# Router logits taken from unscaled rows, the last tile routed alone, and expert loads, gate table and output stores placed anew in a two-layer diffusion backbone block

## The reference, cut to what matters

```
u = modulate(rmsnorm(h, norm_mix[l]), m_lat[0], m_lat[1])
...
h = h + m_lat[2] * y
v = modulate(rmsnorm(h, norm_ffn[l]), m_lat[3], m_lat[4])
lg = (xt @ w_grp + b_grp)
le = (xt @ w_exp + b_exp).reshape(T, N_GROUPS, EXP_PER_GROUP)
...
y = (silu(xb @ w1[e]) * (xb @ w3[e])) @ w2[e]
h = h + m_lat[5] * f
...
return rmsnorm(h, norm_final)
```

## Time and profile before

| | |
|---|---|
| time, median of 3 runs | 2534.87 us (2527.97 to 2536.31) |
| profiled execution: its time, its span | 2530.3 us, 2528.4 us |
| mean granted TensorE clock | 0.973 |
| PE busy | 2361.4 us (93%) |
| DVE, ACT, POOL busy | 1092.6, 338.2, 158.2 us |
| DMA | 574.19 MB, mean 227 GB/s |

### The profile page before, as it was taken

The page is one execution under the profiler, slowest core; times in us unless marked ns, Lnnn a source line. Parts: engine busy times, 40 slices in busy tenths (PEclk is TensorE's granted clock), DMA queues, the critical chain, the costliest instruction groups (busy, mean ns, idle before and its releaser), DMA issues. The chain is left out here.

```text
span 2528.4 us, 32830 instructions
## 1 busy us (share of the span) xinstructions
PE 2361.4 (93%) x14163; PEld 1049.8 (42%) x14164; DVE 1092.6 (43%) x2145; ACT 338.2 (13%) x669; POOL 158.2 (6%) x179
## 2 busy tenths in 40 slices
PE   5999999989999999999999799999999999999991
PEld 3455444544545533333333444444555333333330
DVE  2688377757846422222222453343563222222225
ACT  2210333321011100000000320000120000000001
POOL 2000000001000000000000000000000000000000
PEclk8999999999999999999999899999998999999996
DMA  9567100120120799999999611111019999999975
GB/s 330 200 235 253 34 25 26 47 79 33 67 92 34 299 359 405 405 391 407 392 397 373 223 56 33 50 64 36 34 59 331 387 401 403 404 394 407 387 301 230
DMA packets 186892, 574.19 MB, mean 227 GB/s; under 512 B 14783, under 2 KB 39591, under 8 KB 151544
## 3 DMA queue, kind: packets, MB, share of 16 engines
q1 hardware_dynamic: 168648, 526.48, 54.7%
q0 software_dynamic: 18016, 45.31, 4.7%
q10 hardware_dynamic: 80, 0.26, 0.0%
HBM read 550.74 MB, written 38.03 MB: 233 GB/s over the span
## 5 line engine op out<-in xcount | busy, mean ns | idle before, releaser
L1637 PE MATMUL ps<-arena 128*32 128x512 f32 x6144 | 678.7, 594 | 7.1 <-DMA arena<-in_ex_w_dram 6.5
L1637 PEld LDWEIGHTS ps<-arena 128*32 128x32 f32 x6144 | 193.4, 110 | 423.8 <-issue 423.0
L1663 PE MATMUL ps<-arena 128*32 128x512 f32 x3072 | 338.7, 592 | 5.6 <-DMA arena<-in_ex_w_dram 5.6
L2364 DVE TENSOR_SCALAR arena<-ps,gain_x,mod 128x128 f32<-128x128 f32 x384 | 126.9, 403 | 373.4 <-PE ps L1622 373.4
L1766 PE MATMUL ps<-arena 128*128 128x512 f32 x616 | 264.5, 592 | 0.0
L1507 PE MATMUL ps<-arena 128*128 128x512 f32 x512 | 226.4, 596 | 1.6 <-DVE arena L2166 1.6
L1663 PEld LDWEIGHTS ps<-arena 128*32 128x32 f32 x3072 | 105.1, 110 | 230.1 <-issue 230.1
L2396 DVE SCALAR_TENSOR_TENSOR arena<-ps,arena,gates 128x512 f32<-128x512 f32 x96 | 72.1, 751 | 256.3 <-PE ps L1663 256.3
L1766 PEld LDWEIGHTS ps<-arena 128*128 128x128 f32 x616 | 117.0, 190 | 147.3 <-issue 147.3
L1322 PE MATMUL ps<-arena 128*128 128x512 f32 x384 | 167.3, 593 | 0.7 <-issue 0.7
L2372 DVE TENSOR_TENSOR arena<-arena,ps 128x512 f32<-128x512 f32 x48 | 52.7, 1098 | 239.8 <-PE ps L1637 239.8
(11 more groups left out here) (304 smaller groups left out, 2136.9 us busy)
## 6 DMA issues: line engine op xcount, KB each, us to landing
arena<-in_ex_w_dram SPq DMA_DIRECT2D x384, 1024.0 KB, 11.7
arena<-in_mod_w_dram SPq DMA_DIRECT2D x24, 2048.0 KB, 8.8
arena<-expert_rows SPq DMA_DIRECT2D x16, 1024.0 KB, 8.8
arena<-in_od_w_in_dram SPq DMA_DIRECT2D x12, 1024.0 KB, 5.2
arena<-in_x_dram SPq DMA_DIRECT2D x2, 4096.0 KB, 14.7
normed_rows<-arena POOLq DMA_DIRECT2D x16, 512.0 KB, 2.9
arena<-in_ev_w_in_dram SPq DMA_DIRECT2D x3, 2048.0 KB, 13.6
arena<-in_ev_w_in_dram SPq DMA_DIRECT2D x12, 512.0 KB, 4.1
```

The source lines that it names most:

```text
L1637: ins = nc.tensor.matmul(bank(2 + m)[c:c + n], x[:, j, c:c + n], w_slot(e % 2, m, KC, FE)[:, j], start=j == 0, stop=j == KC - 1)
L1663: ins = nc.tensor.matmul(bank(5 + half)[c:c + n], HT[:, j * P + c:j * P + c + n], w_slot(e % 2, 2, FC, D)[:, j, half * 512:(half + 1) * 51 ...
L2364: ins = V.tensor_scalar(XT[:, b, j * P:(j + 1) * P], bank(j // 4)[:, (j % 4) * P:(j % 4 + 1) * P], gain_x[:, 2 * l + 1, j:j + 1], mod[:, l ...
```

## The change

At the start, tiles 0 and 1 are turned ahead of the fourth modulation matmul (with other PSUM banks for the modulation), and the other tiles one in the middle and one at the end of each tile of v. In routing, PE turns H itself, unscaled, with every eighth element of a row as a chunk; the router's weights are multiplied by the gain once, the shift's part of the logits is added to the router's bias by eight matmuls with ones (`SHIFTED`), and the row's scale is applied to the logits as they are read. ACT makes the scaled rows for the gather table. Logits of tile i-1 stand in the middle of the second half of tile i, their routing ahead of that half's residual; tile 6 is placed before the last tile's transposes are read. In the experts, one weight matrix of expert 0 is loaded before routing, and expert 1's second and third behind the first gather; w2 comes in halves of its inner rows, and the down-projection goes over both column halves in each inner chunk; the gate table is made behind the first pass's gate matmuls; ACT writes half of the first XT. The output stores no longer wait for the last tile's sum. The diff, cut to what carries this (semaphore counts of other norms and a bank number in `rows_to_columns` are left out), outdented by eight:

```diff
@@ -233,6 +233,7 @@
 XN, VTT, SQ_OUT = at(12288, 2, D), at(14336, 2, KC * P), at(16384, 2, D)
+SHIFTED = at(15360, KC, NG + NE)
 HT, SL, HS = at(31232, FE), at(31744, FE), at(30720, FE)
...
@@ -431,6 +432,8 @@
 root_base = [sum(ROOTS[:n]) for n in range(len(ROOTS) + 1)]
+SCALES = [1, 2 * TT, TT, 2 * TT, TT]
+scale_base = [sum(SCALES[:n]) for n in range(len(SCALES) + 1)]
...
@@ -483,6 +486,9 @@
+def halves_before(l, p):
+    return 3 * NP * l + max(3 * p - 1, 0)
+
 def w_slot(b, m, *dims):
...
@@ -524,22 +530,30 @@
                 if m == 2:
-                    cs = slice(half * 512, (half + 1) * 512)
-                    dst = w_slot(e % 2, m, FC, D)[:, :, cs]
-                    src = srcs[m][l, e].rearrange("(p j) n -> p j n", p=P)[:, :, cs]
+                    js = slice(half * 2, half * 2 + 2)
+                    dst = w_slot(e % 2, m, FC, D)[:, js]
+                    src = srcs[m][l, e].rearrange("(p j) n -> p j n", p=P)[:, js]
                 else:
...
+        if l:
+            sp.wait_ge(od_done, 3 * NQ)
+            weights(0, 1)
+        else:
+            sp.wait_ge(hmix_ready, 2 * HC)
+            weights(0, 2)
+        sp.wait_ge(h_ready, 2 * TT * (l + 1))
+        sp.wait_ge(xn_ready, norm_base[2 * l + 2])
         weights(0, 0)
         weights(1, 0)
-        weights(0, 1)
-        weights(0, 2)
+        weights(0, 2 if l else 1)
         sp.wait_ge(lg_mm, TT * (l + 1))
...
         sp.wait_ge(hn_out[1], 16 * (TT // 2) * (l + 1))
+        sp.wait_ge(x_full[0], 16 * (l * NP // 2 + 1))
         weights(1, 1)
...
@@ -548,17 +562,19 @@
                 for m, mm in ((0, up_mm), (1, gate_mm)):
-                    sp.wait_ge(half_mm, 2 * (n0 + p) + m + 1)
+                    sp.wait_ge(half_mm, halves_before(l, p) + m + 1)
                     for e in freed:
...
             if freed_down:
-                for half in range(2):
-                    sp.wait_ge(y_mm, 2 * (n0 + p) - 1 + half)
-                    for e in freed_down:
-                        weights(e, 2, (half,))
+                sp.wait_ge(half_mm, halves_before(l, p) + 3)
+                for e in freed_down:
+                    weights(e, 2, (0,))
+                sp.wait_ge(y_mm, n0 + p)
+                for e in freed_down:
+                    weights(e, 2, (1,))
...
@@ -666,15 +682,12 @@
-        sp.wait_ge(h_ready, 2 * TT * (l + 1))
-        sp.wait_ge(xn_ready, norm_base[2 * l + 2])
         moe_weights(l)
-        sp.wait_ge(y_mm, 2 * NP * (l + 1))
+        sp.wait_ge(y_mm, NP * (l + 1))
         sp.wait_ge(tab_ready, l + 1)
...
         combine(l)
-    sp.wait_ge(cy_used, 2 * TT)
     for i in range(TT):
...
@@ -989,7 +1002,7 @@
     for i in range(TT + CT):
-        nxt = min(3 * (i + 1), TT + CT)
+        nxt = min(2 * i + 3, TT + CT)
         columns(0, lambda i, j: U[:, j, i * P:(i + 1) * P] if i < TT else UC[:, j, (i - TT) * P:(i - TT + 1) * P],
...
@@ -1082,35 +1095,53 @@
         n = 2 * l + 1
-        nb, rb = norm_base[n], root_base[n]
-
-        def columns_of(i):
-            act.wait_ge(xn_T, nb + i + 1)
-            if i >= 2:
-                act.wait_ge(lg_mm, l * TT + i - 1)
-            for j in range(KC // 2, KC):
-                ins = nc.scalar.activation(
-                    VTT[:, i % 2, j * P:(j + 1) * P], bank(5)[:, (j - 4) * P:(j - 3) * P], ACT.Identity,
-                    scale=gain_x[:, n, j:j + 1], bias=mod[:, l, 3, j:j + 1])
-            ins.then_inc(u_act, 1)
-
-        for i in range(TT):
-            if i:
-                columns_of(i - 1)
+        nb, sb_ = norm_base[n], scale_base[n]
+
+        def square(i):
             act.wait_ge(h_ready, 2 * TT * l + 2 * (i + 1))
...
                 .then_inc(sq_done, 1)
-            act.wait_ge(ms_ready, rb + i + 1)
+
+        def root(i):
+            act.wait_ge(ms_ready, sb_ + 2 * i + 1)
             nc.scalar.activation(rstd[:, i:i + 1], rstd[:, i:i + 1], ACT.Sqrt).then_inc(root_ready, 1)
-        columns_of(TT - 1)
+
+        def scaled(i):
+            act.wait_ge(ms_ready, sb_ + 2 * i + 2)
+            if i >= 2:
+                act.wait_ge(hn_out[i % 2], 16 * (l * (TT // 2) + i // 2))
+            nc.scalar.activation(XN[:, i % 2].rearrange("t (c p) -> t p c", p=P),
+                                 H[:, i].rearrange("t (p c) -> t p c", c=KC), ACT.Identity,
+                                 scale=rstd[:, i:i + 1]).then_inc(xn_ready, 1)
+
+        def columns_of(i):
+            act.wait_ge(xn_T, nb + i + 1)
+            if i >= 2:
+                act.wait_ge(lg_mm, l * TT + i - 1)
+            nc.scalar.activation(VTT[:, i % 2, 512:], bank(5), ACT.Copy).then_inc(u_act, 1)
+
+        for i in range(TT):
+            if i:
+                columns_of(i - 1)
+            square(i)
+            if i == TT - 1:
+                columns_of(i)
+            root(i)
+            scaled(i)
         act.wait_ge(gexp_in, 2 * l + 1)
...
     def experts(l):
+        act.wait_ge(x_T, 2 * (l * NP + 1))
+        for j in range(KC // 2, KC):
+            ins = nc.scalar.activation(
+                XT[:, 0, j * P:(j + 1) * P], bank(1)[:, (j - 4) * P:(j - 3) * P], ACT.Identity,
+                scale=gain_x[:, 2 * l + 1, j:j + 1], bias=mod[:, l, 3, j:j + 1])
+        ins.then_inc(xt_ready, 1)
         for p in range(NP):
...
@@ -1192,13 +1223,15 @@
                 g = 32 * (j % 4)
-                ins = nc.tensor.matmul(bank(n % 2)[g:g + 32], SILU32[:, j], w[:, j],
+                ins = nc.tensor.matmul(bank((3, 6)[n % 2])[g:g + 32], SILU32[:, j], w[:, j],
                                        start=j < 4, stop=j >= 4)
...
                 fold(0)
+                for i in range(2):
+                    transposes(0, i, at(41984, 2, D))
         fold(1)
...
@@ -1231,11 +1264,8 @@
         w = slab(L0_V, KC, GV)
-        turned = 0
+        turned = 2
         for i in range(TT + CT):
-            while turned < min(3 * (i + 1), TT + CT):
-                transposes(0, turned, at(41984, 2, D))
-                turned += 1
             if i == 0:
...
@@ -1245,7 +1275,13 @@
                                        start=j == 0, stop=j == KC - 1)
+                if j == 3 and turned < TT + CT:
+                    transposes(0, turned, at(41984, 2, D))
+                    turned += 1
             ins.then_inc(v_mm, 1)
+            if turned < TT + CT:
+                transposes(0, turned, at(41984, 2, D))
+                turned += 1
             if i == 6 or i == 9:
...
@@ -1504,18 +1540,23 @@
             for j in range(KC):
+                if j == KC // 2 and i and half:
+                    logits(i - 1)
                 ins = nc.tensor.matmul(bank(m % 4), mixed[:, j, i * P:(i + 1) * P],
...
         def turn_rows(i):
-            pe.wait_ge(xn_ready, nb + i + 1)
+            pe.wait_ge(h_ready, 2 * TT * l + 2 * (i + 1))
             if i:
...
                 pe.wait_ge(u_act, nb + i)
+            else:
+                for j in range(KC):
+                    nc.tensor.matmul(bank(6)[:, 0:NG + NE], ones, SHIFTED[:, j], start=j == 0, stop=j == KC - 1)
             for j in range(KC):
                 ins = nc.tensor.transpose(bank(4 + j // 4)[:, (j % 4) * P:(j % 4 + 1) * P],
-                                          XN[:, i % 2, j * P:(j + 1) * P], ident)
+                                          H[:, i, j::KC], ident)
             ins.then_inc(xn_T, 1)
...
@@ -1556,24 +1597,21 @@
             out_part(i, 1)
-            if i:
-                logits(i - 1)
             if i >= 2:
                 table_of_rows(i - 2)
+        places(TT - 2)
         pe.wait_ge(h_ready, 2 * TT * (l + 1) - 1)
-        spare(4, 2)
+        spare(2, 2)
         turn_rows(TT - 1)
         spare(4, 2)
-        places(TT - 2)
-        spare(1, 2)
         logits(TT - 1)
         table_of_rows(TT - 2)
-        spare(6, 2)
+        spare(12, 2)
         places(TT - 1)
...
         table_of_rows(TT - 1)
-        spare(6, 2)
+        spare(14, 2)
...
@@ -1657,16 +1695,16 @@
                 pe.wait_ge(y_ready, 2 * (n0 + p))
-            for half in range(2):
-                for j in range(FC):
+            for j in range(FC):
+                for half in range(2):
                     for e, c, n in parts_of(p):
...
                                                start=j == 0, stop=j == FC - 1)
-                ins.then_inc(y_mm, 1)
-
-        table_of_gates(l)
-        spare(2, 2)
+                if j == 1:
+                    ins.then_inc(half_mm, 1)
+            ins.then_inc(y_mm, 1)
+
         turn(0)
...
@@ -1675,6 +1713,7 @@
             else:
+                table_of_gates(l)
                 pe.wait_ge(tab_ready, l + 1)
...
@@ -1851,16 +1890,16 @@
-            V.tensor_copy(MROW[:, n // 2, (n % 2) * 512:(n % 2 + 1) * 512], bank(n % 2))\
+            V.tensor_copy(MROW[:, n // 2, (n % 2) * 512:(n % 2 + 1) * 512], bank((3, 6)[n % 2]))\
...
@@ -2172,6 +2211,11 @@
         dve.wait_ge(small_in, SMALL0 + 64 * l)
+        shape = [P, KC, NG + NE]
+        if l == 0:
```

(63 more changed lines are left out.)

## The result

The changed kernel takes 2544.77 us (median of 13 runs, 2539.41 to 2548.98) against 2533.76 us for the kernel before (13 runs, 2526.15 to 2536.83). The ratio is 1.0051, 95% interval 1.0042 to 1.0059: 0.5% slower, where 2523.8 us and 0.4% faster were forecast. The profiled execution has a span of 2544.2 us, 15.8 more than before.

A forecast was written before the change was run, and what follows sets the result against it. TensorE, busy 93% of the span, was taken as the bound, with the DMA bound nearly on it in the expert passes. Terms summed to -11.1 us, from the median of 2534.87 to 2523.8 us; range 2513 to 2537.

The forecast's parts named there:

- Gate table moved behind the first pass: Experts' first pass: 32 table matmuls lose their free place in the gather's wait; +4.05 us per layer, +8.1.
- The later start of expert 1's last weights only uses up early slack: Expert weight loads: starting expert 1's last weights later was to cost nothing.
- Start: Start up to the value projection: rearranged tile transposes bring later tiles of v sooner; -1.5 us (bounds -4 to +2).
- Loop: Routing loop, PE-bound in both layers: added shift-row matmuls and strided transposes of H; +6.1 us.
- shift matmuls: Routing: eight matmuls with the shift rows, 1.87 us once a layer; +3.7 us.
- strided transposes: Routing loop: transposes of H with every eighth element, +0.15 us per tile; +2.4 us over 16 tiles.
- rival (a): Routing loop: strided transposes cost the fold's price, +12.3 us, total about 2536 us; chance 0.22.
- Tails and landing: Routing's end to first expert pass: gather sooner, -7.0 us; shorter path from its landing to the pass, -2.3.
- Weights' waits: Expert passes: 8 KB runs for down weights remove waits, together -10.4 us; later evictions at each layer's end, +1.3.
- rival (b): Expert passes: the relaid down weights bring nothing and the waits remain, about 2534 us; chance 0.12.
- End: Output stores: a tile leaves while the next is summed, no wait for the last sum; -5.4 us.
- Rival (c): Routing tails: the low clock holds, spares run slow, first pass near 871; +10.8 us a layer, 2545 us; chance 0.06.

The follow-up runs named there:

- run 2: Changed kernel, sync queue only: the four loads of expert 2's first two matrices put ahead of the gate-table wait and the load behind it; 2522.24 us.
- run 1: Changed kernel with the gate table's matmuls and copy back ahead of pass 0's transposes (table early); 2508.23 us, repeated 2507.04 us.
- run 7: Kernel before with only the change's start lines; 2529.40 us, ratio 0.9990 (0.9979 to 1.0002).
- run 8: Kernel before with the third matrix's inner halves, output stores and start changed, without the router's part or order of first expert loads; 2513.12 and 2514.75 us.
- run 9: Table-early kernel (run 1) without the hold of expert 1's second matrix for the first gather; 2509.37 us, against 2507.04 beside it.
- run 3: Kernel before with only the third matrix in inner halves (8 KB runs), the matching down-matmul order and both output halves released together; 2521.84 us.
- runs 4 and 5: Kernel before, third matrix's halves both asked for when the down product is done: column halves (2 KB runs) 2586.75 us, inner halves (8 KB runs) 2549.22 us.
- run 6: Kernel before without the sync engine's wait for the last combined rows ahead of the output stores; 2525.24 us, ratio 0.9969.
- run 10: Table-early kernel (run 1) with 16 filler matmuls instead of 24 between the last tile's logits and its place matmuls; 2510.69 us.

## Why the prediction was wrong

**The step that failed** is "Gate table moved behind the first pass ... +8.1" together with "The later start of expert 1's last weights only uses up early slack". The move was costed on PE and VectorE alone. The same semaphore is waited for in the sync engine's queue, with all later expert loads behind it, and what is late there is not expert 1's weights (they had slack) but expert 2's. That costs 22.5 us (run 2 against the changed kernel), the whole distance from 2522 to 2545. It could have been read in the code beforehand: the load list puts the wait for the table ahead of the loads of pass 1, and the wait becomes late as soon as the table comes after the first freed slot.

**The same step, mis-sized.** From the first up matmul to the hidden's transposes it is +4.0 a layer, as said. But the clock was left out of the table's old place and its new one: 14.0 us by the medians instead of 8.1 (run 2 against run 1).

**Start** (-1.5): -1.9 in the traces of run 7's group, -1.5 at the fifth tile of v in the changed kernel. Right in size; by the time alone (run 7) it is inconclusive. The pause ahead of v did leave half a tile at the lower clock (5.96 us, where the next halves take 3.60), as was feared.

**Loop** (+6.1): from the start of the loop's first output part to the end of its last, run 1 takes 135.29 us, of which 1.87 are logits that lay behind the last part before, so 133.4; run 8, with the old loop, takes 131.7. That is +1.75 in layer 0 and the same in layer 1, together +3.5. The shift matmuls (+3.7) are there; the strided transposes (+2.4) cost nothing, so rival (a) falls.

**Tails and landing** (-7.0 - 2.3 = -9.3): in the kernel with the table early the whole routing part is -8.2 against run 8; less the loop's +3.5 that leaves -11.7. Against the kernel before it is less by the 1.7 that run 8 loses in layer 0's first gather. In the changed kernel 3.6 of it are lost with the table's cover. The emptier queue at the gather, put at some 1 us, shows no gain (run 9).

**Weights' waits** (-10.4 + 1.3): the waits fell by 10.6 in run 3, and rival (b) falls with runs 3 to 5. Run 3 as a whole gave 0.43%, 10.9 us. The 7% between the two rates compared a stretch without the gather (427 GB/s) with one that held it (396); in that stretch, 852 to 857 us, run 3 with 8 KB runs moves 418 GB/s, so like with like differs by some 5%. The page "DMA: Bandwidth & Descriptors" of the Trainium skill (Specifications) has line rate from 512 B up; by it runs 4 and 5 would take the same time, and they differ by 37.5 us.

**End** (-5.4): -5.8 in the trace, -7.8 with an interval of 4.8 to 10.6 in run 6. Right.

**Rival (c)**, the side on which the time came out, wasn't the mechanism: the first pass started at 863.98, not 871. The first 12 and 14 spares ran at the full clock in both layers (5.43 and 6.29 us for 24 and 28 records); only the five behind the gather were slow (4.24 and 3.59 us for ten).

**The account**, in medians: table-early kernel -26 (-25.97 and -26.81), late table +14.0, queue +22.5, sum +10 to +11, measured +11.0. That run 2, without the queue's fault, comes to 2522.24, close to the forecast's 2523.8, is luck in part: the table costs 6 more than its term, and the rest gains 7 more than forecast. The forecast for the same parts without the table was -19.2; the medians put router's part, stores and weights each beyond their terms. The version that keeps the table early beats both kernels, by 1% the one before. To which of its parts the 7 us beyond the forecast belong, the intervals of single runs don't settle.

## What to carry to other kernels

When work is moved, list every engine and queue that waits on its semaphore, and what stands behind each wait: a load queue that issues in order turns one late value into late loads of everything behind. Work that lies free in a wait has more to its worth than its own time: here, moving it out cost that time (8 us), and 6 us more that show as idle while the gather landed and as slower matmuls. Where DMA and compute bounds nearly coincide, both the shape of a load and the moment at which its buffer is given back can be worth tens of microseconds (runs 4 and 5).

## What the hardware showed beyond expectation

Transposes with a stride-eight fp32 stationary operand on 128 partitions ran at the packed rate (1.04 us for eight), though the fold, a plain matmul with that stride, has a step twice as long. The same permutation written by ScalarE is dear: a 128x1024 scaling with permuted output took 2.06 us, a square of the same size with plain output 1.06; VectorE wrote the permuted rows in 1.35 in the kernel before. No run has ScalarE's scaling with plain output, so that the permutation is the cause is inferred. The matmuls behind an idle stretch of 4.7 us in front of the gathered rows ran at the lower clock, and in layer 0 of run 10 those behind 1.19 us too, though not those behind 0.95 us in its layer 1. Idle isn't all of it: in layer 0 of the table-early kernel the transposes took 1.88 with no idle in front, only the table's small matmuls and fillers, and in layer 1 the same sequence took 1.04. What decides between the two, these runs don't show. The first gather of layer 0 took about 9.3 us from issue to use, whether a 2 MB matrix was held back for it or not (changed kernel and run 9), but 8.7 in the kernel before and 10.1 in run 3. That a release later by about 3.5 us cost 27 us even at the better rate was far beyond the expected few; why it weighs so much isn't settled.
